# A decoder layer with product-key experts: the third of eight token blocks moved from whole-table matmuls to gathered rows in both expert stages

## The reference, cut to what matters

```python
q = (xt @ w_pq).reshape(T, H, 2, PEER_HALF)
s = jnp.einsum('thpd,hpkd->thpk', q, sub_keys)
s1, i1 = lax.top_k(s[:, :, 0], K)          # K = 16, of 128 keys
s2, i2 = lax.top_k(s[:, :, 1], K)
cand = (s1[..., :, None] + s2[..., None, :]).reshape(T, H, K * K)
top_s, pos = lax.top_k(cand, K)
g = jax.nn.softmax(top_s)
u = jnp.take(u_tab, ib, axis=0)            # 128 rows a token
a = jax.nn.gelu(jnp.einsum('cd,ced->ce', xb, u)) * gb
vsel = jnp.take(v_tab, ib, axis=0)
y = jnp.einsum('ce,ced->cd', a, vsel)
h = layer_norm(ALPHA * h + y)
```

## Time and profile before

| what | value |
|---|---|
| time, median of 3 runs (lowest, highest) | 3114.03 us (3112.42, 3116.7) |
| the profiled execution's own time | 3114.11 us |
| its span, first to last instruction | 3112.3 us |
| PE, DVE, ACT, POOL busy | 2979.0, 2450.3, 1191.8, 1159.7 us |
| granted clock of PE, mean | 0.984 |

### The profile page before, as it was taken

One profiled execution on the slowest core, in us unless ns is written; L12 is line 12 of the kernel. 1 busy time (PEld: TensorE's weight loads), 2 busy tenths in 40 slices (PEclk: granted clock), 3 DMA queues, 4 the chain that ended last, 5 costly groups with the idle time before them and its releaser, 6 DMA issues. The chain is left out here.

```text
span 3112.3 us, 42565 instructions
## 1 busy us (share of the span) xinstructions
PE 2979.0 (96%) x15866; PEld 2686.6 (86%) x15866; DVE 2450.3 (79%) x4511; ACT 1191.8 (38%) x2213; POOL 1159.7 (37%) x750
## 2 busy tenths in 40 slices
PE   8996998999999999999999999869999999999998
PEld 6886886888999999999999998858888888888887
DVE  4214775455999999999999986569989898999898
ACT  2112332111222466666666656523333333333331
POOL 3222211002656544443444445524434333344331
PEclk9998998999999999999999999989999999999999
DMA  4223222223777666666667677889988888888882
GB/s 172 79 88 132 93 96 82 76 91 114 240 251 255 224 229 239 224 239 243 243 236 240 235 268 280 281 287 314 327 287 307 287 309 307 280 305 297 297 306 78
DMA packets 294024, 695.57 MB, mean 223 GB/s; under 512 B 20432, under 2 KB 136528, under 8 KB 290640
## 3 DMA queue, kind: packets, MB, share of 16 engines
q1 hardware_dynamic: 190928, 316.66, 30.6%
q0 software_dynamic: 73728, 268.47, 25.0%
q10 hardware_dynamic: 29184, 108.01, 9.0%
HBM read 565.13 MB, written 127.93 MB: 223 GB/s over the span
## 5 line engine op out<-in xcount | busy, mean ns | idle before, releaser
L1084 PE MATMUL z_ps<-hT_hi,u_hi 128*128 128x384 f32 x2048 | 703.2, 343 | 18.2 <-POOL u_lo L793 12.7
L1085 PE MATMUL z_ps<-hT_lo,u_hi 128*128 128x384 f32 x2048 | 687.5, 336 | 0.0
L1086 PE MATMUL z_ps<-hT_hi,u_lo 128*128 128x384 f32 x2048 | 687.1, 335 | 0.0
L1393 PE MATMUL y_ps<-v_hi,a_hi 128*128 128x512 f32 x1536 | 600.2, 391 | 24.4 <-DVE y L1521 11.6
L1394 PE MATMUL y_ps<-v_lo,a_hi 128*128 128x512 f32 x1536 | 599.5, 390 | 0.0
L1395 PE MATMUL y_ps<-v_hi,a_lo 128*128 128x512 f32 x1536 | 599.2, 390 | 0.0
L793 POOL TENSOR_TENSOR u_lo<-u_raw,u_hi 128x1024 fp32r<-128x1024 f32 x128 | 315.4, 2464 | 618.2 <-ACT u_hi L789 617.3
L1453 POOL DMA_INDIRECT v_rows<-in_v,room x192 | 286.1, 1490 | 437.8 <-DVE y L1500 414.3
L1084 PEld LDWEIGHTS z_ps<-hT_hi,u_hi 128*128 128x128 f32 x2048 | 387.6, 189 | 20.9 <-POOL u_lo L793 15.3
L1085 PEld LDWEIGHTS z_ps<-hT_lo,u_hi 128*128 128x128 f32 x2048 | 387.6, 189 | 0.0
L1086 PEld LDWEIGHTS z_ps<-hT_hi,u_lo 128*128 128x128 f32 x2048 | 386.6, 189 | 0.0
(11 more groups left out here) (189 smaller groups left out, 4818.7 us busy)
## 6 DMA issues: line engine op xcount, KB each, us to landing
u_raw<-in_uT SPq DMA_DIRECT2D x128, 512.0 KB, 3.7
room<-in_v SPq DMA_DIRECT2D x128, 512.0 KB, 6.3
z<-z_sb ACTq DMA_DIRECT2D x128, 384.0 KB, 5.2
gates<-g_sb ACTq DMA_DIRECT2D x24, 2048.0 KB, 8.8
room<-z SPq DMA_DIRECT2D x16, 1536.0 KB, 9.0
z_in<-z SPq DMA_DIRECT2D x16, 1536.0 KB, 8.2
g_in<-gates SPq DMA_DIRECT2D x16, 1536.0 KB, 17.5
room<-gates SPq DMA_DIRECT2D x15, 1536.0 KB, 17.9
```

The source lines that it names most:

```text
L1084: nc.tensor.matmul(o, u_hi[e][:, k], hT_hi[:, k, cols], start=(k == 0), stop=False)
L1085: nc.tensor.matmul(o, u_hi[e][:, k], hT_lo[:, k, cols], start=False, stop=False)
L1086: last = nc.tensor.matmul(o, u_lo[e][:, k], hT_hi[:, k, cols], start=False, stop=(k == KT - 1))
L1393: nc.tensor.matmul(o, ah, v_hi[p][:, i, c], start=(i == 0), stop=False)
```

## The change

Three edits come together. (1) A third block is treated by rows in both expert stages: `GB = UB = 3`, `DB = 5`. A z tile then has 640 columns instead of 768; they are cut into a half of 384 (`z_first`) and one of 256 (`z_rest`, one PSUM bank shared by both tiles in flight). `PER_TURN` is a new table with a sum of 384. Since blocks 0 and 1 are both searched in `score` now, the search inside `experts_in` covers six turns (0 to 5) instead of seven, and gate steps stand in turns 3 to 7. (2) The block of `h` that the dots use is copied once to PSUM (`h_ps`), and the dots read it there. (3) The two one-hots of a gate step are one instruction of 1024 elements. In `score`, ACT takes over the copies out of PSUM that DVE made, and DVE searches the head before for two blocks. The found indices are kept twice (`b % 2`).

```diff
-GB = 2
+GB = 3
 DB = TB - GB
 DT = DB * P
+UB = 3
+ZB = TB - UB
+ZT = ZB * P
...
                 def turn(h):
-                    last = h == PH - 1
-                    query(h, 0)
-                    if not last:
+                    if h:
+                        search(h - 1, 0)
+                    if h < PH - 1:
                         split_w(h + 1, 0)
-                    scores(h, 0)
-                    query(h, 1)
-                    if not last:
+                    if h:
+                        search(h - 1, 1)
+                    if h < PH - 1:
                         split_w(h + 1, 1)
...
-    HT = DT // 2
+    CUT = ZT - 2 * P
...
-    PER_TURN = [28, 40, 27, 27, 27, 27, 27, 53]
+    PER_TURN = [24, 46, 56, 38, 38, 38, 72, 72]
...
-        h_own = [sb(f"h_own{b}", [P, D]) for b in range(2)]
-        z_ps = [[bank(f"z_ps{e}{a}") for a in range(2)] for e in range(2)]
+        h_own = sb("h_own", [P, D])
+        z_first, z_rest = [bank(f"z_first{e}") for e in range(2)], bank("z_rest")
+        z_ps = [[z_first[e][:, 0:CUT], z_rest[:, e * 2 * P:(e + 1) * 2 * P]] for e in range(2)]
+        h_ps = ctx.enter_context(nc.psum_tensor("h_ps", [P, D], F32))
...
                     if a == 0:
-                        pe.wait_ge(u_lo_in[e], 2 * m + j + 1)
-                        wait(pe, z_read[e], 2 * (2 * m + j))
-                    cols = slice(GB * P + a * HT, GB * P + (a + 1) * HT)
+                        pe.wait_ge(u_lo_in[e], i + 1)
+                        wait(pe, z_read[e], 2 * i)
+                    else:
+                        wait(pe, z_read[1 - e], 2 * ((tile + 1) // 2))
+                    cols = slice(UB * P, UB * P + CUT) if a == 0 else slice(UB * P + CUT, T)
...
-                    for hot, side in ((hot2, 1), (hot1, 0)):
-                        last = nc.vector.tensor_tensor(hot[g][:], bc(iota_ps, 1, 4), bc(iT[:, side, t0:t0 + 4], 2, NK),
-                                                       ALU.is_equal)
-                    last.then_inc(hot_in[g], 1)
+                    nc.vector.tensor_tensor(hot[g][:], bc(bc(iota_ps, 1, 4), 1, 2), bc(iT[:, :, t0:t0 + 4], 3, NK),
+                                            ALU.is_equal).then_inc(hot_in[g], 1)
...
                     if slot == 0:
-                        v.wait_ge(h_here[b], 16)
-                    wait(v, row_used, i)
-                    nc.vector.tensor_tensor_reduce(rows_in[r][:], rows_in[r][:], h_own[b][:], 1.0, 0.0, ALU.mult, ALU.add,
+                        v.wait_ge(h_here, 16 * (i // (PH * TOPK) + 1))
+                        link(nc.vector.tensor_copy(h_ps[:], h_own[:]))
+                        nc.vector.engine_nop().then_inc(h_taken, 1)
+                    nc.vector.tensor_tensor_reduce(rows_in[r][:], rows_in[r][:], h_ps[:], 1.0, 0.0, ALU.mult, ALU.add,
                                                    ahead.z_rows[:, b, slot:slot + 1]).then_inc(row_used, 1)
```

More of the change, by code:

```diff
@@ L1124, in scale_hot @@
                     for t in range(4):
-                        last = nc.scalar.activation(hot1_g[g][:, t], hot1[g][:, t], ACT.Copy,
+                        last = nc.scalar.activation(hot1_g[g][:, t], hot[g][:, 0, t], ACT.Copy,
                                                     scale=gT[:, t0 + t:t0 + t + 1])
@@ L1149, in _ @@
-                        act.wait_ge(z_done[e], 2 * (2 * m + j) + a + 1)
+                        tile, a = s * SLOTS // 2 + k // 2, k % 2
+                        e, i = tile % 2, tile // 2
+                        if a == 0 and tile < NK - 1:
+                            split_u(tile + 1)
+                        act.wait_ge(z_done[e], 2 * i + a + 1)
                         if a == 0:
-                            wait(act, z_stored[e], 16 * (2 * m + j))
-                        nc.scalar.activation(z_sb[e][:, a * HT:(a + 1) * HT], z_ps[e][a][:, 0:HT],
-                                             ACT.Copy).then_inc(z_read[e], 1)
+                            wait(act, z_stored[e], 16 * i)
@@ L1161, in _ @@
-                        if s < TB - 1 and k == SLOTS - 2:
-                            act.wait_ge(gaps, s + 2)
-                            tk.exp().then_inc(exps, 1)
+                            act.wait_ge(z_read[e], 2 * i + 2)
+                            act.dma_start(d["z"][tile], z_sb[e][:]).then_inc(z_stored[e], 16)
+                        if s == 0 and k in (1, 3):
+                            act.wait_ge(gaps, k // 2 + 1)
+                            tk.exp(k // 2).then_inc(exps, 1)
@@ L1164, in _ @@
+                        if s < TB - 2 and k == SLOTS - 2:
+                            act.wait_ge(gaps, s + 3)
+                            tk.exp(s + 2).then_inc(exps, 1)
+                        if UB > GB and s == TB - 2 and k == SLOTS - 6:
+                            act.wait_ge(row_used, 2 * PH * TOPK)
+                            nc.scalar.activation(kept[:, 2], ahead.z_rows[:, GB], ACT.Gelu).then_inc(late_gelu, 1)
                         for step in steps_at(s, k):
@@ L1291, in _ @@
                             dot(i)
+                        if UB > GB and s == TB - 2 and k == SLOTS - 2:
+                            v.wait_ge(late_gelu, 1)
+                            link(nc.vector.tensor_tensor(kept[:, 2], kept[:, 2], ahead.picked_g[:, GB], ALU.mult))
+                            nc.vector.engine_nop().then_inc(found_in, 1)
                         if s == TB - 1:
-                            for t in range(DB):
+                            for t in range(ZB):
                                 if PRODUCTS_AT[t] == k:
@@ L1430, in _ @@
                 hi(0, DB - 1)
-                nc.scalar.activation(a_rows[:], ahead.z_rows[:], ACT.Gelu).then_inc(rows_gelu, 1)
+                nc.scalar.activation(a_rows[:], ahead.z_rows[:, 0:GB], ACT.Gelu).then_inc(rows_gelu, 1)
                 for r in range(1, NG):
```

334 lines of the change are left out of this document (178 added, 156 removed).

## The result

The changed kernel takes 3308.61 us (median of 4 runs, 3300.8 to 3313.31); the kernel before, run beside it, 3114.53 (3112.42 to 3116.7). The ratio is 1.062, interval 1.0599 to 1.0642: slower by 6.2%, where the forecast was 1.1% and the upper end of its range 3235 us. The profiled execution has a span of 3299.0 us against 3112.3.

What follows compares the result with a forecast made beforehand. PE set the pace, with DVE and DMA close behind; the change lowers PE's load and raises the other two. -70 + 41 + 70 - 8 = +33 on 3112.3 us; forecast 3147 us, slower by 1.1%, range 3020 to 3235.

Steps and rivals of the forecast that it cites:

- what PE gives back, DVE takes. And then the rows: `experts_out`: DVE needs 32.4 us a round where PE needed 32.7; gathered rows then make it 35.0.
- turns 0 to 5: `experts_in`: DVE's need sets the pace, 866 us where 936 were taken before, -70 us.
- turns 6, 7: `experts_in`: gathered rows limit, at 2.62 us a row for turn 6; 189 and 198 us, +41 us.
- a round: `experts_out`: 35.0 us, between 32.4 (nothing waits) and 37.5 (each step waits for its landing); +70 over 30 rounds.
- at 93 to 97% busy they take 124, 128, 143: `experts_in`, early turns: DVE's needs divided by that utilisation, with 3 x 157 more, give 866 us.
- the queue that the prediction described for turns 6 and 7: POOL in `experts_in`: when a gather waits, the next low part of `u` waits behind it, and PE for that.
- The check by bytes: Turn 6: 59.7 MB in 189 us is 316 GB/s, about the highest that any 100 us show, 321.
- -8 for rounds 0 and 31: `experts_out`: these two rounds have no rows and stay with PE, -8 us.
- bursts of three rows: `experts_out`: three rows in a block's step of 6.4 us ask a landing within 6.4 us or less of the ring of four.
- Rival C: Each step with doubles waits for a landing: turns 6 and 7 at 215 us each, rounds 37.5; 3265 us, chance 0.17.
- Rival B: Throughput alone limits, latency not: 345 GB/s, turns 6 and 7 at 173 and 184 us, rounds 33.1; 3060 us, chance 0.20.
- `score` at nothing: `score`: the second search adds 7 to 11 us to a DVE turn, covered by PE, so no cost.

Runs made afterwards that it cites:

- experiment 5: Changed kernel with rings of 4 and 6 row buffers instead of 3 and 4, and gathers of 512 of 1024 values: 3054.68 us.
- experiment 6: Changed kernel with only the first three rows gathered in `experts_in`, all dots reading them without waiting, and a ring of 5 in `experts_out`: 3024.45 us.
- experiment 3: Changed kernel with the last dense block multiplied twice in each round (144 matmuls instead of 120) and a flat table of rows in `experts_in`: 3296.97 us.
- experiment 1: Changed kernel with longer rings, 4 row buffers instead of 3 in `experts_in` and 6 instead of 4 in `experts_out`: 3109.32 us, 0.998 of the kernel before.

## Why the prediction was wrong

The direction was right, and so was the mechanism for the last two turns and the rounds: "the rows are" the limit in turns 6 and 7, and in `experts_out` "what PE gives back, DVE takes. And then the rows". For turns 0 to 5 it was wrong: there the prediction had next to no cost for gathers.

| term | forecast | changed kernel | what the experiments show |
|---|---|---|---|
| turns 0 to 5 | 866 us (-70) | 946 (+14: cut at the same matmuls, these turns took 932 before, and not the prediction's 936) | 865 without gathers, 903 with a ring of 4 |
| turns 6, 7 | 189, 198 | 206, 204 | 181, 186 with a ring of 4; 160, 165 with half rows as well |
| a round | 35.0 us | 36.26 | 34.24 with 5 buffers, 32.80 with 6 |
| `experts_out` in all | +62 | +108 | +4 with a ring of 6 |

**Turns 0 to 5: the step that failed, and the largest, 80 us.** DVE's need was right: the prediction's needs add up to 833 us, and DVE was busy 831 in these turns. Without gathers they take 864.6 us, close to the forecast, though with luck in the sum: turns 1, 2, 4 and 5 took 4 to 5 us less each than forecast, turn 3 took 15 more. What failed is "at 93 to 97% busy they take 124, 128, 143": I took the utilisation from stretches of the kernel before with 27 to 40 rows a turn, and applied it to 38 to 56. The only allowance for gathers was "56 rows begin to press". At that density each short group of dots meets the same ring of three as in turns 6 and 7, and DVE was busy only 88% of the time. The views name a row for 40 us of the idle time before the dots of turns 1 to 5, and none ("issue") for 34.5. By the semaphore times, 75 of the 78 us of idle time before those dots end within 0.35 us of the landing of the dot's own row: both kinds are waits for rows. A ring of 4 gives back 44 of the 80 us. Of the other 38 us (902.7 against 864.6), part is DVE's own work becoming longer while POOL issues gathers. One small group in turn 2, with longer rings and half rows (experiment 5), then without gathers (experiment 6):

```profile
L741 DVE TENSOR_TENSOR room<-top 128x256 f32<-128x256 f32 x8 | 12.2, 1527 | 0.0
```

```profile
L741 DVE TENSOR_TENSOR room<-top 128x256 f32<-128x256 f32 x8 | 3.4, 420 | 0.0
```

DVE is busy 146 us in the one and 134 in the other, 12 of the 17 us by which the turns differ (155.7, 138.9). In the former PE also waits 29.3 us for `u_lo` on POOL in that turn, and POOL 60.2 for dots: the queue that the prediction described for turns 6 and 7, now in an early turn. How much of the 38 us each of the two makes over all six turns is open.

**Turns 6 and 7: mis-sized by 17 and 6 us.** The term was 2.62 us a row. The prediction's own working, 2.16 and 0.6 for the longer landing, makes 2.76, which it didn't take in full for turn 6; measured are 206.1 / 72 = 2.86 and 2.83. Two of its seven dots in the earlier trace rows had no wait for a row before them, so 2.51 and 2.16 were means over a stretch that was not all ring. The check by bytes (316 GB/s, "about the highest") did not bind (the kernel before reached 327 in 2115 to 2215 us, not only 321): the turns ran at 286 and 308 GB/s, and at 326 and 339 with one buffer more.

**The rounds: mis-sized by 1.3 us of 35.** The measured round lies within the bounds (32.4 and 37.5), and the lower one is where a ring of 6 ends. I took the middle. Of the -8 for rounds 0 and 31 only 4 came, and round 1 grew by 6.5 us instead of 2.3. The rows' cycle, worked out from the semaphore times of 353 rows (2200 to 3200 us), is 11.3 us from the end of an addition to the end of the one four rows later: 0.8 until the gather is issued, 7.5 until it has landed, 1.8 in which the row lies ready, 1.3 for the addition. 139 of these rows were waited for. So a ring of four would do in the mean (12.8 rows x (7.5 + 1.3) / 4 is 28 us a round); what costs the time, by my reading, is that the additions come two or three together, as the prediction's "bursts of three rows" had it. No run placed the additions otherwise within a round, so that part is not shown. Rival C, "the burst rule bites in full" (3265 us), came nearest: its 37.5 was too high by 1.2, its turns 6 and 7 by 9 and 11.5, and it kept the wrong term for turns 0 to 5, without which it would have been 3265 + 80 = 3345. It had 0.17. The clock did fall, to 0.90, but experiment 3 speaks against its remark that this would add to the time, in the rounds at least. Rival B put 345 GB/s as the limit without latency; experiment 1 shows that it was a fair picture of the machine, 350 GB/s at a share of 0.98, and the wrong one for a ring of four, where the share was 0.90. The Trainium skill (DMA: Bandwidth & Descriptors, "Where 436 GB/s comes from") puts one core's limit of HBM at about 358 GB/s; the 350 of experiment 1 agree with it as a sustained value, more than the single slices above 400 let me think.

**Right**: dots of 1.21 to 1.23 us, none above (384 of them); the single one-hot at 1.22; `score` at nothing (the stage after it starts 3.9 us earlier); PE's relief worth nothing. **Mis-sized**: one instruction for two one-hots saves 0.146 us and not 0.06.

The range failed for the reason that the forecast did: turns 0 to 5 had no bad case at all, not even in C, and half of C was cut off its upper end. Landing times were not the reason. By the semaphore times their median is 7.6 us in the rounds, as before the change, and 6.2 and 6.4 in turns 6 and 7.

## What to carry to other kernels

A ring can't give rows faster than buffers over (landing + use), the landing counted from the start of the issue. That is only a bound: here it would allow 28 us for a round that took 36.26. Work it out for the burst and not for the mean, with the rows as dense as the change will make them, and for every stage, not only for the one that already waits. Before giving an engine's spare time to gathered rows, try one or two more buffers first: here they were worth 6%, as much as the change lost. And a utilisation read from a stretch is a property of its waits, not of the engine; in turn 6 DVE is busy 62% of the time, and 90% with the same dots and no gathers (experiment 6):

```profile
1606.50:1748.30 141.80, 141.80 (x1028) 141.51 (x1028) 127.28 (x184) 99.76 (x209) 38.27 (x16) 1.00 0.43 156
```
